# Adding expert rows to X inside the gathering DMA, and a rearranged LayerNorm behind the experts, in a two-layer decoder trunk

## What is computed

```python
x = layer_norm(ALPHA * x + h, ln_mix_g[layer], ln_mix_b[layer])
f = moe(x, router_w, router_bias, ...)          # 16 experts, each token uses two
x = layer_norm(ALPHA * x + f, ln_ffn_g[layer], ln_ffn_b[layer])

# in moe, with w_sel normalised to sum 1 over the two chosen experts:
for e in range(N_EXPERTS):
    h = silu(xt @ w_gate[e]) * (xt @ w_up[e])
    y = y + combine[:, e:e + 1] * (h @ w_down[e])
```

## Time and profile before

| | |
|---|---|
| Median of 3 runs (range) | 1360.01 us (1358.62 to 1363.75) |
| The profiled execution: its time | 1359.62 us |
| Its span, first to last instruction | 1358.1 us |
| PE busy | 1231.4 us, 91% |
| DVE busy | 996.6 us, 73% |
| ACT busy | 726.7 us, 54% |
| POOL busy | 251.6 us, 19% |
| Experts' middle part, layer 0 | 460 to 715 us, PE busy 252.7 of 255 |
| Experts' middle part, layer 1 | 1030 to 1285 us, PE busy 252.87 of 255 |

### The profile page before, as it was taken

One profiled execution on the slowest core, in us unless ns is written; L12 is line 12 of the kernel. 1 busy time (PEld: TensorE's weight loads), 2 busy tenths in 40 slices (PEclk: granted clock), 3 DMA queues, 4 the chain that ended last, 5 costly groups with the idle time before them and its releaser, 6 DMA issues.

```text
span 1358.1 us, 16965 instructions
## 1 busy us (share of the span) xinstructions
PE 1231.4 (91%) x6689; PEld 1038.2 (76%) x6689; DVE 996.6 (73%) x1293; ACT 726.7 (54%) x850; POOL 251.6 (19%) x256
## 2 busy tenths in 40 slices
PE   7999978888899599999999779989977999999993
PEld 7989967775587488888888379978856888888871
DVE  3965345543666699889997875459676999899988
ACT  4443222222233378888886233676234888888852
POOL 4432343210500100011003110343001000110032
PEclk8999979997998699999999879999977999999997
DMA  6322050003134599999996522120355999999961
GB/s 178 127 77 79 1 161 1 1 1 117 40 116 163 208 390 420 412 414 414 414 406 254 178 101 63 63 109 21 140 223 216 401 411 415 415 414 416 397 229 70
DMA packets 76113, 294.52 MB, mean 217 GB/s; under 512 B 8176, under 2 KB 34505, under 8 KB 51200
## 3 DMA queue, kind: packets, MB, share of 16 engines
q1 hardware_dynamic: 64704, 252.51, 48.2%
q0 software_dynamic: 7296, 26.22, 5.4%
q10 hardware_dynamic: 4032, 14.68, 2.7%
HBM read 266.50 MB, written 26.89 MB: 216 GB/s over the span
## 4 chain that ended last, share of the span: by engine, by line
PE 77%; DVE 14%; ACT 3%; issue 2%; DMA 2%; POOL 2%; SPq 0%; POOLq 0%; DVEq 0%; ACTq 0%
PE bank L1116 12%; PE bank L1118 12%; PE bank L1117 12%; PE bank L667 5%; PE bank L668 5%; PE bank L1022 3%; PE bank L1024 3%; PE bank L1023 3%; PE bank L1110 2%; PE bank L712 2%; PE bank L713 2%; PE bank L1073 2%; DVE X L2284 1%; PE bank L788 1%; PE bank L1145 1%
## 5 line engine op out<-in xcount | busy, mean ns | idle before, releaser
L2070 DVE TENSOR_TENSOR UNIT_LOW<-work,UNIT_HIGH 128x2048 fp32r<-128x2048 f32 x192 | 436.9, 2289 | 51.1 <-ACT UNIT_HIGH L1287 50.4
L1287 ACT ACTIVATE UNIT_HIGH<-work 128x2048 fp32r<-128x2048 f32 x192 | 366.4, 1919 | 84.6 <-PE bank L1118 83.5
L1116 PE MATMUL bank<-UNIT_HIGH,XGT_HIGH 128*128 128x512 f32 x512 | 204.4, 399 | 5.0 <-DVE XGT_LOW L2239 5.0
L1118 PE MATMUL bank<-UNIT_HIGH,XGT_LOW 128*128 128x512 f32 x512 | 201.1, 393 | 0.0
L1117 PE MATMUL bank<-UNIT_LOW,XGT_HIGH 128*128 128x512 f32 x512 | 200.8, 392 | 0.0
L2633 POOL DMA_INDIRECT work<-x_rows,idx_all x32 | 41.4, 1292 | 569.7 <-PE bank L1110 410.5
L1287 ACT ACTIVATE work<-bank 128x512 f32<-128x512 f32 (+3 forms) x178 | 74.4, 472 | 107.0 <-PE bank L781 29.4
L1116 PEld LDWEIGHTS bank<-UNIT_HIGH,XGT_HIGH 128*128 128x128 f32 x512 | 97.3, 190 | 25.1 <-DVE XGT_LOW L2239 5.8
L1118 PEld LDWEIGHTS bank<-UNIT_HIGH,XGT_LOW 128*128 128x128 f32 x512 | 96.9, 189 | 21.0
L1117 PEld LDWEIGHTS bank<-UNIT_LOW,XGT_HIGH 128*128 128x128 f32 x512 | 97.1, 190 | 19.4
L1116 PE MATMUL bank<-UNIT_HIGH,HT_HIGH 128*128 128x512 f32 x256 | 99.8, 390 | 1.1 <-DVE HT_LOW L2251 1.1
(11 more groups left out here) (492 smaller groups left out, 2696.4 us busy)
## 6 DMA issues: line engine op xcount, KB each, us to landing
work<-in_moe_w_gate_dram SPq DMA_DIRECT2D x64, 1024.0 KB, 7.4
work<-in_moe_w_up_dram SPq DMA_DIRECT2D x64, 1024.0 KB, 7.5
work<-in_moe_w_down_dram SPq DMA_DIRECT2D x64, 1024.0 KB, 8.0
y_rows<-work ACTq DMA_DIRECT2D x28, 512.0 KB, 8.1
work<-in_ab_w_in_dram SPq DMA_DIRECT2D x10, 1024.0 KB, 5.4
work<-in_c_w_in_dram SPq DMA_DIRECT2D x8, 1024.0 KB, 5.4
x_rows<-X SPq DMA_DIRECT2D x8, 512.0 KB, 2.6
X<-in_x_prompt_dram SPq DMA_DIRECT2D x4, 512.0 KB, 5.1
```

Source lines behind the costliest of these rows:

```text
L1116: mm(to, x[0], high, start=start, stop=False)
L1118: return mm(to, x[1], high, start=False, stop=stop)
L1287: return nc.scalar.activation(out, in_, ACT.Copy, scale=scale)
L2070: V.tensor_tensor(UNIT_LOW[home(l, n)][:, :], work[:, UNIT * home(l, n):UNIT * home(l, n) + UNIT], UNIT_HIGH[n % HIGHS][:, :].bitcast(F32) ...
```

## The change

Four things are changed together.

1. The weight of a row is applied where the row leaves PSUM: `result(e)` copies with a scale that is a column of `w_slot` (for each slot of each expert the weight of its token). `w_slot` is made in routing by ten more matmuls behind the ten of L1098 and one more DVE product, `WEIGHT_HOT`. For the late experts the scale stays 1.
2. The ten gathering DMAs write into X itself with `compute_op=ALU.add`. They are issued for all tiles with k = 0, then for all tiles with k = 1, each of these after the k = 0 DMA of its tile has arrived. The ten DVE additions and the `y_homes` go. A token whose choice is a late expert now reads a row of zeros, which is written once near the start. POOL also waits until ACT has scaled X.
3. The norm behind the experts: `mean(t)` adds PSUM to X with the row's sum as a by-product, ACT takes the sum of squares and the root in `spread_root(t)`, and DVE applies gain, root and bias in two passes, `normalised(t)`. ACT's scaling pass, the statistics passes and POOL's bias pass go.
4. `combine` gets four pairs of banks, so only its fifth tile waits. SP's wait for `ysel_in[3]` ahead of mixer1's loads goes. The branch for more than 128 tokens at one expert (`overflow`) is changed to match; it isn't taken with these inputs.

```diff
+        SQUARES = work[:, 12288:12288 + D]
+        COMBINE_BANKS = ((0, 1), (2, 3), (4, 7), (5, 6), (0, 1))
...
             def mixer1():
-                sp.wait_ge(ysel_in[3], 32)
...
+                        sp.dma_start(w_list[l].rearrange("(p n) o -> p (n o)", p=P), zero_i[:, :].bitcast(F32))\
+                          .then_inc(lists_zeroed, 16)
+                        zero_rows = zero_i[:, 0:2 * D // P].bitcast(F32)
+                        sp.dma_start(y_rows[l][LATE[0]:NE, :].rearrange("e (p c) -> (e p) c", c=2 * D // P), zero_rows)\
+                          .then_inc(lists_zeroed, 16)
...
+                pe.wait_ge(slot_hot, 3 * l + 3)
+                for k in range(2):
+                    for t in range(NT):
+                        last = mm(bank[7][:, 0:NE], SLOT_HOT[0:ROWS[t], k, t, :].bitcast(F32), WEIGHT_HOT[0:ROWS[t], k, t, :],
                                   start=(k == t == 0), stop=(k == 1 and t == NT - 1))
                 last.then_inc(idx_ps, 1)
...
                 for t in range(NT):
-                    if t >= 2:
-                        pe.wait_ge(norm_sum, q * NT + t - 1)
+                    if t == NT - 1:
+                        pe.wait_ge(norm_sum, q * NT + 1)
                     for j, e in enumerate(LATE):
                         pe.wait_ge(y_out_sb, NE * l + e + 1)
                         for half in range(2):
-                            last = mm(bank[2 * (t % 2) + half][0:ROWS[t], :], LATE_COLS[:, j, tile_cols(t)],
+                            last = mm(bank[COMBINE_BANKS[t][half]][0:ROWS[t], :], LATE_COLS[:, j, tile_cols(t)],
...
+                def spread_root(t):
+
+                    r, n = ROWS[t], q // 2 * NT + t + 1
+                    w = lnw[0:r, t, :]
+                    act.wait_ge(norm_stats, q * NT + t + 1)
+                    nc.scalar.activation(SQUARES[0:r, :], X[0:r, t, :], ACT.Square, bias=w[:, 2:3], accum_out=w[:, 3:4])\
+                        .then_inc(norm_square, 1)
+                    act.wait_ge(norm_square, n)
+                    nc.scalar.activation(w[:, 14:15], w[:, 3:4], ACT.Sqrt, scale=1.0 / D, bias=eps_col[0:r, :])\
+                        .then_inc(norm_root, 1)
...
                 for t in range(NT):
-                    root(t)
-                    if t:
-                        scaled(t - 1)
+                    spread_root(t)
                     if q == 1 and t >= 3:
                         x1_rounded(t - 3)
-                scaled(NT - 1)
...
                 def result(e):
                     act.wait_ge(unit_used, NU * l + down_unit(e, 1) + 1)
                     at_least(act, y_stored[e % 2], y_arrivals(l, e // 2))
+                    scale = 1.0 if e in LATE else w_slot[:, e:e + 1]
                     for c in range(2):
-                        last = copy(YO[e % 2][:, 512 * c:512 * c + 512], bank[5 + c][:, :])
+                        last = copy(YO[e % 2][:, 512 * c:512 * c + 512], bank[5 + c][:, :], scale)
...
+                def mean(t):
+
+                    r, n = ROWS[t], q * NT + t
+                    x, w = X[0:r, t, :], lnw[0:r, t, :]
+                    dve.wait_ge(ysel_in[t], 32 * (l + 1))
+                    dve.wait_ge(out_ps, n + 1)
+                    for half, b in enumerate(COMBINE_BANKS[t]):
+                        c = slice(512 * half, 512 * half + 512)
+                        last = V.scalar_tensor_tensor(x[:, c], x[:, c], 1.0, bank[b][0:r, :], ALU.mult, ALU.add,
+                                                      accum_out=w[:, half:half + 1])
+                    last.then_inc(norm_sum, 1)
+                    dve.wait_ge(norm_sum, n + 1)
+                    V.tensor_scalar(w[:, 2:3], w[:, 0:1], w[:, 1:2], -1.0 / D, ALU.add, ALU.mult).then_inc(norm_stats, 1)
+
+                def normalised(t):
+
+                    r = ROWS[t]
+                    x, w = X[0:r, t, :], lnw[0:r, t, :]
+                    dve.wait_ge(norm_stats, q * NT + t + 1)
+                    dve.wait_ge(norm_square, l * NT + t + 1)
+                    mine(V.scalar_tensor_tensor(x, x, w[:, 2:3], gain[0:r, :], ALU.add, ALU.mult))
+                    dve.wait_ge(norm_root, q * NT + t + 1)
+                    mine(V.reciprocal(w[:, 14:15], w[:, 14:15]))
+                    mine.settle()
+                    V.scalar_tensor_tensor(x, x, w[:, 14:15], bias[0:r, :], ALU.mult, ALU.add).then_inc(norm_done, 1)
...
-                stats(0)
+                mean(0)
                 for t in range(NT):
                     if t + 1 < NT:
-                        stats(t + 1)
-                    coefficients(t)
-                    if t:
-                        finish(t - 1)
+                        mean(t + 1)
+                    normalised(t)
                     if q == 1 and t >= 3:
                         x1_split(t - 3)
-                finish(NT - 1)
...
+                V.tensor_tensor(WEIGHT_HOT, oh, wsel[:, 0:2, :].unsqueeze(3).broadcast_to([P, 2, NT, NE]), ALU.mult)\
+                    .then_inc(slot_hot, 1)
...
                 places_of_late(l)
+                dve.wait_ge(idx_ps, 2 * l + 2)
+                V.tensor_copy(w_slot[:, :], bank[7][:, 0:NE]).then_inc(idx_ready, 1)
                 split_unit(l, EARLY_SPLITS)
...
-                dve.wait_ge(late_act, (NT + 1) * l + NT)
-                for t, ys in enumerate(y_homes(l)):
-                    dve.wait_ge(ysel_in[t], 32 * (l + 1))
-                    for k in range(2):
-                        x = X[0:ROWS[t], t, :]
-                        mine(V.scalar_tensor_tensor(x, ys[k][0:ROWS[t], :], wsel[0:ROWS[t], k, t:t + 1], x, ALU.mult, ALU.add))
-                        mine.settle()
...
                 def select(rows):
-                    for t, ys in enumerate(y_homes(l)):
-                        if t >= 2:
-                            pool.wait_ge(unit_used, NU * l + NU - RING + t - 1)
-                        for k, to in enumerate(ys):
+                    for k in range(2):
+                        for t in range(NT):
+                            if k:
+                                pool.wait_ge(ysel_in[t], 32 * l + 16)
                             pool.indirect_dma_start(
-                                out=to[0:ROWS[t], :], out_offset=None, in_=rows,
+                                out=X[0:ROWS[t], t, :], out_offset=None, in_=rows, compute_op=ALU.add,
                                 in_offset=bass.IndirectOffsetOnAxis(ap=pos_i[0:ROWS[t], k, t:t + 1], axis=0),
                             ).then_inc(ysel_in[t], 16)
...
+                pool.wait_ge(late_act, (NT + 1) * l + NT)
...
-                pool.wait_ge(lnp_in[1], 32 * (l + 1))
-                for t in range(NT - 1):
-                    pool.wait_ge(gained, l * (NT - 1) + t + 1)
-                    G.tensor_tensor(X[:, t, :], X[:, t, :], LNP[:, 1, 1, :], ALU.add).then_inc(norm_done, 1)
```

More of the change, by code:

```diff
@@ L95, in hybrid_trunk @@
         slot_list = [nc.dram_tensor(f"slot_list{l}", [SLOTS, 1], I32).ap() for l in range(2)]
+        w_list = [nc.dram_tensor(f"w_list{l}", [SLOTS, 1], F32).ap() for l in range(2)]
         y_rows = [nc.dram_tensor(f"y_rows{l}", [SLOTS, D], F32).ap() for l in range(2)]
@@ L319, in hybrid_trunk @@
                      [xt_flat[:, 4096 + P * t:4224 + P * t] for t in range(NT - 1)] + [lnp_free[:, 1792:1920]]]
[L321 to L325, removed]
+        WEIGHT_HOT = view(27776, (2, NT * NE)).rearrange("p k (t e) -> p k t e", t=NT)
+        W_ALL = view(13312, (BLOCKS, NE))
+        W_CUR = work[:, 13392:13393]
         own = {e: sem(f"{e}_own") for e in ("dve", "pool")}
@@ L2082, in stats @@
                         c = slice(512 * half, 512 * half + 512)
-                        last = V.scalar_tensor_tensor(x[:, c], x[:, c], 1.0 if q % 2 else ALPHA,
-                                                      bank[2 * (t % 2) + half][0:r, :], ALU.mult, ALU.add)
+                        last = V.scalar_tensor_tensor(x[:, c], x[:, c], ALPHA, bank[2 * (t % 2) + half][0:r, :],
+                                                      ALU.mult, ALU.add)
                     last.then_inc(norm_sum, 1)
@@ L2100, in coefficients @@
                         .then_inc(norm_coef, 1)
+                gain, bias = LNP[:, q % 2, 0, :], LNP[:, q % 2, 1, :]
                 def finish(t):
                     r = ROWS[t]
-                    gain, bias = LNP[0:r, q % 2, 0, :], LNP[0:r, q % 2, 1, :]
-                    dve.wait_ge(norm_scaled, q * NT + t + 1)
-                    last = V.tensor_tensor(X[0:r, t, :], X[0:r, t, :], gain, ALU.mult)
-                    if q % 2 and t < NT - 1:
-                        last.then_inc(gained, 1)
-                        return
@@ L2110, in finish @@
-                    mine(last)
-                    if q % 2:
-                        dve.wait_ge(norm_done, q * NT + t)
-                    mine.settle()
-                    V.tensor_tensor(X[0:r, t, :], X[0:r, t, :], bias, ALU.add).then_inc(norm_done, 1)
```

(21 more changed lines are left out.)

46 lines of the change are left out of this document (28 added, 18 removed).

## The result

The changed kernel takes **1392.83 us** (median of 4 runs, 1391.8 to 1393.53) against 1360.49 for the kernel before on the same chip: ratio 1.0227, 95% interval 1.0199 to 1.0254. So it is slower clear of noise, by about 2%. The forecast was 1346, in a range of 1340 to 1358. Its profiled execution has a span of 1391.3 us, 33.2 more than before.

The account below looks back on a forecast made before the run. PE bounds most of the kernel (77% of the chain), DVE 14%, taking over behind both layers' experts. Gains 8.5 + 7.5, less 1.5 and 0.3, make 14.2: 1360.0 to 1346 us, range 1340 to 1358.

Parts of the forecast that it names:

- Part 4: Small things: routing 0.3 us for both layers; weighted copies and the zeros and lists stored near the start cost nothing.
- the adding DMAs as the bound: Rival: DVE's wait for gathers in mean(t) sets the end; slower, 1371 at three times the plain price; chance 0.12.
- DVE sets the pace behind the experts, from mean(1) on: Behind both layers' experts, DVE waits for PE's tile 1, 7.03 us after combine starts, then is never short of work.
- 4.55 a tile: New norm on DVE: mean 1.75 us plus normalised 2.8, above PE's 3.55; gains 7.5 in layer 1, 8.5 in layer 0.
- The adding gather costs 2.9 us for 512 KB at full share: Gathers into X behind the experts: plain gather 1.64 us plus 1.3 for reading X; bounds 1.64 and 4.2.
- c_w_in's contention: Layer 0: the 3 MB load, issued 3.4 us earlier, shares DMA engines with the last gathers; 1.5 us lost, between 0 and 3.
- a landing of tile 0's second gather later than 9 us after its issue: Sign of being wrong, for the adding gathers behind the experts: tile 0's second lands over 9 us after issue.
- Routing costs 0.3: In routing, ten more matmuls may show 0.4 us; DVE's extra product is hidden; counted as 0.3 for both layers.
- The weighted copies hide behind ACT's 0.69 of room: In the experts, a copy takes 0.688 instead of 0.590 us, 0.2 per expert, hidden by ACT's idle 0.69: nothing lost.
- SP's wait and the banks: Removing SP's 3.4 us wait issues c_w_in earlier, causing contention; four pairs of banks let combine deliver tiles every 3.55 us.
- Tables: ACT's squares and roots in the new norm follow each other without table loads, so tables don't alternate.
- a table load between a square and its root: Sign of being wrong, for ACT in the new norm: table loads stand between squares and roots.

Follow-up runs that it names:

- b_small: The kernel before plus the change's four small stores near the start, large stores kept over all 128 partitions: 1361.76 us against 1361.90, ratio 0.999.
- b_127: The kernel before with each large store of finite rows cut into partitions 1 to 127 and partition 0: 1415.25 us, ratio 1.0403.
- b_124: The kernel before with each large store of finite rows cut into partitions 4 to 127 and the first four: 1362.9 us against 1360.55.
- a_banks: The changed kernel with its finite-row stores split into 112 and 15 partitions, and combine's four PSUM banks put back: 1340.01 us, ratio 0.9825.
- a_split: The changed kernel with each store of finite rows over partitions 1 to 127 split into 112 and 15 partitions: 1339.77 us, ratio 0.9837.
- b_126: The kernel before with each large store of finite rows cut into partitions 1 to 126, 0 and 127: 1361.47 us against 1360.55.

## Why the prediction was wrong

**The step that failed** is the last of Part 4: "The zeros and lists near the start are a few more issues on SP, which waits for PE between weight loads there: nothing." It put a price on the small stores, and these do cost nothing (b_small, 0.999). What it left out is that the same lines of the diff change the shape of two large stores that were already there, from 128 partitions to 127. b_127 has only that, with one small store for each layer, and is 55 us slower than before. The cover that I named, SP's wait for PE between weight loads, was there: SP issued its next load at 52.41 before, 9.8 us after its last store. But what counts is when the load lands. ACT needed it at some 76.8, 34 us after the stores' issue. Stores that still run between 60 and 65, as in b_124, fit into that; stores of 77 us don't. None of the rivals was this one; the slower one, the adding DMAs as the bound, did not happen.

**The rest, point by point.**

- *DVE sets the pace behind the experts, from mean(1) on.* Right. Start at 7.13 after `combine`, forecast 7.03.
- *4.55 a tile.* The mechanism held, the size was 0.50 too large: 4.05 a tile. Of this 0.28 are in `mean` (1.47 from its start to that of `normalised`, forecast 1.75): reading out a row's sum takes DVE 0.08 and overlaps the next addition (the row at 1369.74 above), where I had taken 0.15 each. The other 0.21 are in `normalised` (2.59, forecast 2.8), whose operations overlap a little too. Over four means and five normalised tiles that is 2.2 us: forecast were 7.5 in layer 1 and 8.5 in layer 0, measured 9.6 in layer 1, and in layer 0 10.8 with and 11.1 without the wait for the DMA.
- *The adding gather costs 2.9 us for 512 KB at full share.* Measured 2.92. Of the 1.5 that I had taken off for c_w_in's contention, layer 0 shows 0.2. I had named a landing of tile 0's second gather later than 9 us after its issue as a sign of being wrong: in layer 0 it took 9.8 (8.8 in layer 1), and DVE's mean(0) behind it was put down to PE all the same. By the half rate of the Trainium skill ("Collectives: The Full Stack", section "The bandwidth ceiling: the fold count and why AG ≠ RS ≠ AR") it would be 3.3, an estimate: nearer than the plain 1.64, and 0.4 too much here.
- *Routing costs 0.3.* The totals can't show it: between kernels the front differs by 2.6 us (746.61 to 749.25 at `combine`), more than this term. In the traces the way from the first of the ten matmuls to the first use of the gathered rows is 7.37 and 8.12 us in the two layers before and 7.44 and 7.77 after: nothing to be seen, though the ten matmuls took 4.78.
- *The weighted copies hide behind ACT's 0.69 of room.* Right: 677 ns for one, 590 without the weight, and PE is busy 252.94 of 255 us in the middle part of layer 0's experts (513 to 768), where it had 252.7.
- *SP's wait and the banks.* I took the banks for a gain of no size of its own, and so they were (a_banks, 1340.01). Taking SP's wait away was expected to cost contention; beyond the 0.2 above nothing of it is seen in the tails.
- *Tables.* They don't alternate, but I had named a table load between a square and its root as a sign of being wrong, and one stands there in each tail, ahead of the first root: 1.28 at 808.71 and at 1368.57. It runs beside DVE's wait ahead of mean(1), and no wait for ACT follows, so it costs nothing.

With the stores' shape left as it was, the sum is the 1346 that I gave, and a_split came to 1340. Of the 6 between them some 4.3 come from the shorter `mean` and `normalised` (two layers) and 1.5 from the contention that I had taken off and a_split doesn't show; the rest is within the spread of its runs. The gain in layer 0 is also one against a kernel with a late gather there: against b_127's 40.84 it would be 7 in place of 11.

## What to carry to other kernels

Read every DMA in a diff for its shape, above all one that only lost a row: on how many engines it runs hangs on how the outermost size divides (127, 124 and 126 here), and cutting one partition off 128 made 1 MB take some 38 us (an estimate, 1.04 MB at 27 GB/s). When an issue on a queue takes 19 us, look at the transfer issued ahead of it, and take the DMA share in sixteenths. Ask of a load not only when it was issued but when it landed. And cut both spans at common events before explaining anything: here the total hid a gain of 20 behind a loss of 53.

## What the runs showed of the hardware

- A large store on one DMA engine moves 27 GB/s, and behind it the issues of SP's own queue take 19 us each, three in the changed kernel, though each had but 8 or 40 KB. In b_127 the second pair of stores took 22.78 to issue, the first weight load behind it came 34 us late, at 86.41, and took 42.12 to land: PE stood still there too. In both kernels the load landed at 128.3 to 128.5, whenever it was issued.
- PE's granted clock was 0.55 behind an idle time of 4.13 us and 1.00 behind one of 1.54, in the same place of two kernels that differ little. The same 24 records took 13.3 to 13.8 us behind idle times of 4.1 to 4.6 (before, b_124, b_small), 12.41 behind 2.82 and 2.69 (b_126, and b_127 in layer 1) and 10.71 behind 1.54 and 2.12.
- A row sum as by-product: 0.08 us on DVE, overlapped; on ACT, with the square, 0.19 more.
- POOL takes 1.54 us to issue an adding gather in the steady part and 0.94 for a plain one.
